# Four landing buffers in place of five for the weight loads of a SwiGLU stage

## The reference, cut to what matters

```python
h = rms_norm(x, ffn_norm_g[layer])
x = x + (jax.nn.silu(h @ w_ffn_gate[layer]) * (h @ w_ffn_up[layer])) @ w_ffn_down[layer]
return rms_norm(x, final_norm_g)
```

## Time and profile before

| | |
|---|---|
| median of 3 runs | 378.76 us (378.25 to 379.41) |
| the profiled execution, own time | 379.42 us |
| its span, first to last instruction | 377.1 us |
| PE busy | 367.2 us (97%) |
| PEld busy | 308.6 us (82%) |
| DVE busy | 323.9 us (86%) |
| ACT busy | 227.7 us (60%) |
| POOL busy | 40.2 us (11%) |
| mean granted TensorE clock | 0.997 |
| moved by transfers | 74.80 MB, mean 198 GB/s |

### The profile page before, as it was taken

One profiled execution on the slowest core, in us unless ns is written; L12 is line 12 of the kernel. 1 busy time (PEld: TensorE's weight loads), 2 busy tenths in 40 slices (PEclk: granted clock), 3 DMA queues, 4 the chain that ended last, 5 costly groups with the idle time before them and its releaser, 6 DMA issues. The chain is left out here.

```text
span 377.1 us, 4744 instructions
## 1 busy us (share of the span) xinstructions
PE 367.2 (97%) x1847; PEld 308.6 (82%) x1847; DVE 323.9 (86%) x376; ACT 227.7 (60%) x263; POOL 40.2 (11%) x41
## 2 busy tenths in 40 slices
PE   6999999999999999999999999999999999999993
PEld 5998888788888888888888888888888888888782
DVE  3999995989867999989769759999999999999625
ACT  4759588676174966546447436955683692687204
POOL 2698020000000104000100000100100100000002
PEclk9999999999999999999999999999999999999998
DMA  7889065946180393899727911794795498361003
GB/s 277 253 276 314 13 214 171 325 174 222 26 310 0 53 334 123 314 357 324 265 71 262 364 44 48 179 381 179 182 359 234 132 313 337 111 236 44 0 0 112
DMA packets 41293, 74.80 MB, mean 198 GB/s; under 512 B 2316, under 2 KB 14648, under 8 KB 41272
## 3 DMA queue, kind: packets, MB, share of 16 engines
q1 hardware_dynamic: 38944, 70.03, 53.1%
q0 software_dynamic: 2112, 4.19, 6.5%
q10 hardware_dynamic: 216, 0.28, 0.2%
HBM read 73.46 MB, written 1.05 MB: 198 GB/s over the span
## 5 line engine op out<-in xcount | busy, mean ns | idle before, releaser
L1086 DVE TENSOR_TENSOR w_lo<-w_raw,w_hi 128x2048 fp32r<-128x2048 f32 x33 | 75.4, 2296 | 10.4 <-ACT w_hi L696 10.2
L969 ACT ACTIVATE w_hi<-w_raw 128x2048 fp32r<-128x2048 f32 x33 | 62.7, 1912 | 24.4 <-DVE w_raw L1534 24.4
L696 ACT ACTIVATE w_hi<-w_raw 128x2048 fp32r<-128x2048 f32 x33 | 62.6, 1912 | 21.6 <-DMA w_raw<-in_w_in 10.3
L1554 DVE TENSOR_TENSOR w_lo<-w_raw,w_hi 128x2048 fp32r<-128x2048 f32 x33 | 74.6, 2284 | 0.2 <-ACT w_hi L969 0.2
L1685 PE MATMUL pp<-w_hi,yT_hi 128*128 128x512 f32 (+1 forms) x104 | 40.5, 390 | 0.0
L1687 PE MATMUL pp<-w_lo,yT_hi 128*128 128x512 f32 (+1 forms) x104 | 40.3, 387 | 0.0
L1686 PE MATMUL pp<-w_hi,yT_lo 128*128 128x512 f32 (+1 forms) x104 | 40.3, 387 | 0.0
L1685 PE MATMUL pp<-w_hi,hT 128*128 128x512 f32 x96 | 38.0, 396 | 0.0
L1687 PE MATMUL pp<-w_lo,hT 128*128 128x512 f32 x96 | 37.4, 390 | 0.0
L1686 PE MATMUL pp<-w_hi,hT 128*128 128x512 f32 x96 | 37.4, 389 | 0.0
L2067 PE MATMUL pa<-w_hi,hT 128*128 128x512 f32 x64 | 25.0, 391 | 0.2 <-DVE region_a L1577 0.2
(11 more groups left out here) (340 smaller groups left out, 782.7 us busy)
## 6 DMA issues: line engine op xcount, KB each, us to landing
w_raw<-in_w_in SPq DMA_DIRECT2D x20, 1024.0 KB, 5.3
w_raw<-in_w_ffn_gate SPq DMA_DIRECT2D x11, 1024.0 KB, 8.7
w_raw<-in_w_ffn_up SPq DMA_DIRECT2D x11, 1024.0 KB, 8.0
w_raw<-in_w_ffn_down SPq DMA_DIRECT2D x11, 1024.0 KB, 7.7
w_raw<-in_w_o SPq DMA_DIRECT2D x4, 1024.0 KB, 5.8
x_sb<-in_w_ffn_gate POOLq DMA_DIRECT2D x3, 1024.0 KB, 9.2
w_raw<-in_w_out_attn SPq DMA_DIRECT2D x2, 1024.0 KB, 9.6
w_raw<-in_w_out_mlstm SPq DMA_DIRECT2D x2, 1024.0 KB, 5.2
```

What stands on the lines that cost most here:

```text
L696: nc.scalar.activation(w_hi[:, slot_of(c), :], early_raw(c), ACT.Copy).then_inc(hi_ready, 1)
L969: nc.scalar.activation(w_hi[:, slot_of(c), :], form_raw(name, p), ACT.Copy).then_inc(hi_ready, 1)
L1086: nc.vector.tensor_tensor(w_lo[:, slot_of(c), :], early_raw(c), w_hi[:, slot_of(c), :].bitcast(F32), ALU.subtract).then_inc(lo_ready, 1)
L1554: nc.vector.tensor_tensor(w_lo[:, slot_of(c), :], form_raw(*FORM[c]), w_hi[:, slot_of(c), :].bitcast(F32), ALU.subtract).then_inc(lo_ready, 1)
```

## The change

The plan no longer has buffer 4. The list of buffers loses its last entry, the one that comes free with the numerators, and the choice goes over four buffers in place of five, for the loads and for the final gain at the end. The region `w_raw4` and its semaphore are still declared and are not used. Nothing else differs: the same loads in the same order, the same arithmetic, the same order on each engine.

```diff
-    free = [(2 * c, "lo", c + 1) for c in last] + [(2 * C_FFN + 3, "normed", 4), (2 * C_FFN - 9, "num", H_M)]
-    value = [EARLY[c][1] // 16 for c in last] + [0, 0]
+    free = [(2 * c, "lo", c + 1) for c in last] + [(2 * C_FFN + 3, "normed", 4)]
+    value = [EARLY[c][1] // 16 for c in last] + [0]
     where = {}
 
     def place(name, p, use):
-        buf = min(range(RAW + 2), key=lambda n: free[n][0])
+        buf = min(range(RAW + 1), key=lambda n: free[n][0])
...
-    buf = min(range(RAW + 2), key=lambda n: free[n][0])
+    buf = min(range(RAW + 1), key=lambda n: free[n][0])
     return where, (buf, *free[buf][1:])
```

## The result

The changed kernel takes 384.11 us (median of 3 runs, 384.06 to 384.18) against 378.76 before: a ratio of 1.0143, 95% interval 1.0112 to 1.0175. The forecast was 385.3, between 382.0 and 388.5, slower. The profiled execution took 384.18 us, its span is 382.4. Four single executions in the runs further down took 1.3 to 2.1 ms, one of them of the kernel before; they are left out of the ratios.

A forecast was written before the change was run, and what follows sets the result against it. PE and DVE were taken to run full and in step, so DVE's stalls for late B21 in sets 0 to 2 add 3.15 + 1.75 + 1.6 = 6.5 us to the 378.76 median: 385.3 us, range 382.0 to 388.5.

The forecast's parts named there:

- The plan: SP's queue: every load waits for what its successor waited for; 29 loads and the final gain move, no instruction added.
- Landing in the successor's place: B21 of sets 0 to 2, issued behind the adding transfer, lands 9.7, 8.7 and 8.6 us after issue.
- The three DVE waits: DVE at L1554 waits for ACT's high part, held by late B21: about 3.3, 1.8 and 1.7 us.
- B11 and NG2: Loads that come later: B11 of sets 1 to 3 by 3.4 us, NG2 making ACT 1.2 late; both cost 0.
- DVE's delay becomes the kernel's: Between 226 and 350 us, each us DVE loses, less some tenths, lengthens the kernel; 6.5 us in all.
- B21 of set 3: The last set's B21 load has no adding transfer and keeps its time, adding nothing to the sum.
- The sum against the median: Whole kernel: 6.5 us takes the profiled 379.42 to 385.9; less its 0.66 above the median, 385.3.
- PE's gaps and the clock: PE idle at turn L2033 by 2.9 us, then about 1.7 twice; granted clock 1.00 until the last matmul.
- the fall: Rival: PE's idle gap at the turn drops the clock to 1.2 GHz, adding 2.7 or 5.5 us; chance 0.07.
- Hidden: Rival: B21 lands in time, served beside the adding transfer, so not slower, 378.8 us; chance 0.07.
- only the first burst: Rival: B21 costs time only in set 0, quicker landing hides sets 1 and 2; 381.9 us, chance 0.10.
- A slower landing: Rival: B21 and adding transfer delay one another, up to 9.7 us landing in each set; 387.4 us, chance 0.08.

The follow-up runs named there:

- set 0 alone: Against the kernel before, all five buffers kept and only the load of B21 of set 0 held back (lo 44): 382.00 us, ratio 1.0100.

## Why the prediction was right, point by point

*The plan.* Each load's wait moved up by one place, and SP's issues show it. Right.

*Landing in the successor's place.* 9.7, 8.7, 8.7 us against 9.7, 8.7, 8.6 assumed. Right, and this was the term that no row before could show. That B21 and the adding transfer read the same bytes changed nothing that these numbers show.

*The three DVE waits.* 3.27, 1.76, 1.72 us measured, 3.35, 1.8, 1.7 forecast. B11 and NG2 cost nothing, as said.

*DVE's delay becomes the kernel's.* From DVE's last residual ahead of the feed-forward part (L1273 at 195.53 before, 194.31 after) to PE's last T4 (350.41, 355.81 after) the time grew by 161.50 - 154.88 = 6.62 us, against 6.5 forecast. The stretch is right to 0.1.

*B21 of set 3.* The forecast let it keep its time. It did not: SP issued it at 311.75 us before and at 329.64 after. It landed 5.2 us later, and no DVE wait followed, so it cost nothing, as the sum had it.

*The sum against the median.* It came out at 5.35 us, 1.2 less. The step that was off is the base. The prediction took off 0.66 us for a profiled execution above the median, but its trace was slower by more than that outside the stretch that changed: it reached 195.53 in its first part, the one after 194.31, and another 0.64 us lies behind the last T4 and outside the span (6.62 - 1.22 - 0.64 = 4.76, the difference of the two profiled executions). The plans do not differ up to the load of chunk 37 at 181 us, and the 1.3 us were there earlier: SP's first load of the feed-forward part is issued at 164.38 before and 163.08 after. Over all twelve traces the end of the first part lies between 194.3 and 195.5. Why it scatters, no run shows. The run with only B21 late, which keeps all five buffers, lost 5.8 us against its own runs of before.

*PE's gaps and the clock.* I forecast 2.9 and twice about 1.7 us and a clock of 1.00; there were 2.81, 0.13 and 1.50, and the clock fell. The faulty step was to take the 3.8 us of idle PE after the last matmul as a sign that a shorter gap is safe. As a rival the fall had its place but the wrong price: 2.7 us or more on top, where the trace of set 0 alone has 1.53. In the changed kernel the next DVE wait covered it, and that the sum held in spite of the wrong clock is luck. Of the runs with only B21 late, three with a mean clock of 0.998 took 383.98 to 384.12 us, one at 0.992 took 384.71: a fall costs there little or nothing.

*Hidden* and *only the first burst* fell with the landing times. *A slower landing* did not occur.

## What to carry to other kernels

Where two engines run full in step, a buffer is worth the waits at the one tight place, not a share of the traffic: here one buffer in five carried three loads, and 26 others did not need it. When a load's release moves, look at what is already in the queues at the new time; the landing is best read from the load that stood there. And a stall on one engine can pay for a loss on another (here about 1.4 us), so add up only what nothing else covers.

## What the runs showed of the hardware

- A plain load of 1 MB issued 2 us behind an adding transfer of 1 MB got no packet through for 3.8 us, against some 1.1 us with no adding transfer, and issued 3.4 us later still it landed at the same moment (247.8 and 247.9).
- The adding transfer needs 8.5 to 10.2 us beside one or more loads, 12.8 when it comes second; the same bytes copied without adding, in packets twice as large, 5.6.
- The granted clock fell with a gap of PE of 2.81 us (with one of 2.5 in the trace of set 0 alone, a good us after PE was back at work), not with gaps of 1.5 and 1.6; yet it held for 3.8 us after the last matmul.
